# Moving the convolution steps of VectorE behind the masked copies in the recurrent heads

## The chip, the cores and the metric

One Trainium2 chip, of which the kernel uses one core. TensorE (PE) multiplies matrices into PSUM, VectorE (DVE), ScalarE (ACT) and GpSimd (POOL) do the elementwise work, and each engine works through its own list of instructions in the order in which the program wrote it; engines wait for one another through semaphores. The metric is device time in microseconds (us) of one execution; less is better.

## The reference, cut to what matters

Two transformer-like blocks on 1024 tokens of width 1024. The change touches the recurrent heads of the first block, eight heads of dimension 128, a gated delta rule in both directions of time:

```
qkv = silu(conv5(h @ w_in[:, q|k|v]))          # 5-tap convolution over time, per channel
q, k = l2norm(q), l2norm(k)
a_kk = strict_lower(kb @ k.T * gam)             # per chunk of 64 tokens
sol  = solve(a_kk + I, [v*beta, kb*exp(gc)])    # unit lower triangular
for chunk in chunks:                            # the scan
    v_new = u - w @ state
    o     = (q*exp(g)) @ state + a_qk @ v_new
    state = state*exp(g_last) + k.T @ v_new
out = rmsnorm(o) * silu(z)
```

The projections `h @ w_in` are by far the largest part of TensorE's work here.

## The kernel before, in words

The heads are worked through in 16 **halves**, numbered s = 2h + part: half s inverts the triangular matrices of four of the eight chunk pairs of head h. Meanwhile the same half prepares the next head (projections of q and k in an even half, of v and z in an odd one, their convolutions and norms), and runs scan steps of a head that is inverted. For the next heads 1 to 4 a half also projects gate columns of a later stage: in halves 0 to 7 (called **long** here) the preparation has 24 steps instead of 16; halves 8 to 13 are **short**; halves 14 and 15 prepare no head.

The inversion goes by levels. Level 0 sets up: TensorE multiplies k with k and q (L684), VectorE makes the matrix MT (L1178), TensorE transposes it (L694), and VectorE makes the two **masked copies** of level 0, called XT0 (L1183) and X0 (L1185), and then the masked attention product aq (L1192, two instructions). Level n = 1 to 6 then does, each step needing the one before:

- TensorE: product Y (L701), which needs X(n-1); ScalarE copies it out, Yb (L991)
- TensorE: product XT (L707), which needs Yb; ScalarE copies it out, Xb (L996)
- VectorE: first masked copy XTn (L1202)
- TensorE: transposes (L713), which need Xb; VectorE: second masked copy Xn (L1206)

The other work of VectorE in a half: the five convolution steps of each of q, k, v (one L1099 and four L1102 of 128x1024; the last of them signals `conv_sum`), then the final step (L1108), which needs ScalarE's tanh of the sum (L838) and signals `conv_out`, for which TensorE's flips (transposes, L644) wait; a split of loaded weights (L228, "ck" below) for which the next projection waits; z's product (L1114); the steps of the scan (L1219, L1227, L1237, L1240); and at the end of a head `fin`: a tiny L1247, which needs eight squares made by ScalarE (L1026), then GpSimd's power (L1329) and product (L1332), TensorE's transposes (L764), and VectorE's z0 and z1 (L1254), which free PSUM bank 5.

The order of the work on each engine is fixed when the program is built. `merged` interleaves the threads of a half (inv, prep, scan, fin, dec) by their number of steps, and `walk` issues one step of a thread's generator at each key of that list. All engines walk the same list:

```
for order in plan:
    walk(order, make)
```

So step i of "prep1" on ScalarE stands at the place of step i of "prep1" on VectorE, wherever the other threads' steps are. In an odd long half ScalarE's list reads: gate tanh (L860), tanh of k's convolution (L838, waits for `conv_sum` of k), from half 3 on the eight squares (L1026), then Yb of level 1 (L991), a copy of weights (L223), Xb of level 1 (L996). In an odd short half the tanh of k stands behind Xb of level 1.

Of the kernel before, what the change touches and what calls it, by code (L numbers as in the profile page):

```python
# [88 lines left out]
def walk(order, make):  # L89

    live = {}
    for key in order:
        if key not in live:
            live[key] = make(key)
        next(live[key], None)
    for g in live.values():
        for _ in g:
            pass


def idle(n):
    for _ in range(n):
        yield
# [17 lines left out]
def program(nc, x, wst, wab, cwt, vecs, gate, relb, meta, lam, lruw, cst, onehot, rope, msk, out):  # L121
    with ExitStack() as ctx:
# [654 lines left out]
        def both(first, second):  # L777
            yield from first
            yield from second
# [350 lines left out]
        def dve_prep0(v, h):  # L1130
            if h in GATES:
                yield from dve_next(v, CK[h, "g0"], h - 1)
            yield from dve_next(v, CK[h, "q"], h - 1 if h and h not in GATES else None)
            yield from conv_steps(v, h, "q", chq[h % 2])
            dve_ck(v, CK[h, "k"] + 1)
            yield
            yield

        def dve_prep1(v, h):
            q = h % 2  # L1140
            v.wait_ge(prep_ev, (h, "fq", 1))
            v.do.tensor_scalar(qe[h % 3], ssq[q], 128.0 * EPS, 128.0 * EPS * EPS, ALU.mult, ALU.add).then_inc(*dve_step.tick())
            yield from conv_steps(v, h, "k", chk[q])
            dve_ck(v, CK[h, "g1" if h in GATES else "v"] + 1)
            yield
            yield
            if h in GATES:
                yield from dve_next(v, CK[h, "v"])

            for n, _ in enumerate(conv_steps(v, h, "v", vf)):  # L1150
                if n == 0:
                    v.wait_ge(prep_ev, (h, "fk", 1))
                    v.do.tensor_scalar(ssk[q], ssk[q], 1.0, EPS, ALU.mult, ALU.add).then_inc(*unit_v.tick((h, "eps")))
                if n == 2:
                    v.wait_ge(gate_v, "beta")
                    v.wait_ge(gate_a, "egl")
                    v.wait_ge(unit_pow, h)
                    v.do.tensor_tensor(nk[q], ssk[q], rk, ALU.mult)
                    v.do.tensor_tensor(rk, rk, rk, ALU.mult).then_inc(*dve_step.tick())
                    v.wait_ge(dve_step, dve_step.n)  # L1160
                    for d in range(2):
                        v.do.tensor_tensor(br[q][d], gt["beta"][:, :, d * 8 + h], rk, ALU.mult).then_inc(*dve_step.tick())
                    v.wait_ge(dve_step, dve_step.n)
                    for d in range(2):
                        o = v.do.tensor_tensor(db[q][d], gt["dec"][:, :, d * 8 + h], br[q][d], ALU.mult)
                    o.then_inc(*unit_v.tick((h, "set")))
                yield
            dve_ck(v, CK[h, "z"] + 1)
            yield
            yield  # L1170
# [72 lines left out]
        def dve_fin(v, h):  # L1243
# [6 lines left out]
            for hf in range(2):  # L1250
# [3 lines left out]
                v.do.scalar_tensor_tensor(out=z, in0=bank(5), scalar=vc[:, NORMA:NORMA + 1], in1=z, op0=ALU.mult, op1=ALU.mult).then_inc(*fin_z.tick((h, hf)))  # L1254
                yield

        def dve_delta(v):
            def make(key):
                what, *of = key
                if what == "prep":  # L1260
                    return both(dve_prep0(v, 0), dve_prep1(v, 0))
                if what == "bias":
                    return idle(1)
                return {"qk": dve_qk0, "fill": dve_fill, "gates": dve_gates, "prep0": dve_prep0, "prep1": dve_prep1, "inv": dve_inv, "scan": dve_scan, "fin": dve_fin, "split": dve_first_split, "dec": lambda v, *_: idle(3)}[what](v, *of)

            for order in plan:
                walk(order, make)

# [2156 lines left out]
        @block.vector  # L3427
        def _(vector):
            v = Engine(vector)
            dve_input(v)  # L3430
            dve_delta(v)
            stage_ends(v, "dve", 1)
            dve_dilated(v)
            stage_ends(v, "dve", 2)
            dve_branches(v)
            stage_ends(v, "dve", 3)
            dve_rows(v)
            dve_ff(v)
            dve_lru(v)
            stage_ends(v, "dve", 6)  # L3440
            dve_rope(v)
            stage_ends(v, "dve", 7)
            dve_values(v)
            stage_ends(v, "dve", 8)
            dve_diff(v)
# [173 lines left out]
```

## Time and profile before

| | us |
|---|---|
| runs without the profiler, median of 3 | 3379.44 (3375.18 to 3379.78) |
| the profiled execution's own time | 3371.57 |
| its span, first to last instruction | 3369.8 |
| TensorE busy in the span | 3160.2 (94%) |
| VectorE busy | 1500.1 (45%) |
| ScalarE busy | 1054.8 (31%) |
| GpSimd busy | 361.4 (11%) |
| mean granted TensorE clock | 0.969 of full |

The page gives busy time of each engine, the waits say who waited for whom, the timeline lists instructions in order of time (runs of like ones merged), with the idle time before an instruction and what ended it in brackets, and the windows give busy time and granted clock of a stretch. The heads take the stretch from about 119 us to 1085 us. Matmul ends are modelled, so a busy TensorE isn't one at its peak; its idle time is real.

### The profile page before, as it was taken

To read this page: it belongs to the slowest core of one execution; us is meant where nothing else is said; L and a number is where in the kernel's file an instruction comes from. 1 tells how busy PE (TensorE), PEld (TensorE's weight loads), DVE (VectorE), ACT (ScalarE), POOL (GpSimd) and SP (SyncE) were. 2 spreads that over 40 slices of the span, in tenths; PEclk is the share of its full clock that TensorE was granted. 3 is DMA by queue.
4 is the path that set the end of the run, shared out by engine and by line. 5 is a ranking of instruction groups with operands and counts; after the bars stand their busy time and mean duration, and the time that the engine had idled before them with its cause. 6 is when DMAs were issued, how large, how long until landed. Compare 5 with 4: busy or idle time off the path is not lost.

```text
span 3369.8 us, 38831 instructions
## 1 busy us (share of the span) xinstructions
PE 3160.2 (94%) x16207; PEld 2575.5 (76%) x16207; DVE 1500.1 (45%) x2112; ACT 1054.8 (31%) x2290; POOL 361.4 (11%) x433
## 2 busy tenths in 40 slices
PE   7999999898899988989989999999999999998997
PEld 5788888777777877777744788888888877777876
DVE  4456556565643122121123345444444668533452
ACT  3544444444442223222300132222211333213452
POOL 0222232223221000000010000000000111001111
PEclk9999999999999999999999999999999999997998
DMA  2211111101111111101351321111111320111010
GB/s 105 66 55 45 48 48 45 32 32 38 32 38 57 57 35 49 49 29 44 122 206 67 150 73 57 50 42 46 50 51 50 107 78 26 62 38 45 26 39 26
DMA packets 59313, 194.86 MB, mean 58 GB/s; under 512 B 7649, under 2 KB 15329, under 8 KB 49410
## 3 DMA queue, kind: packets, MB, share of 16 engines
q1 hardware_dynamic: 58272, 191.29, 16.4%
q8 instruction: 128, 2.10, 0.3%
q10 hardware_dynamic: 866, 1.09, 0.1%
q14 instruction: 47, 0.39, 0.0%
HBM read 158.37 MB, written 33.98 MB: 57 GB/s over the span
## 4 chain that ended last, share of the span: by engine, by line
PE 80%; DVE 10%; ACT 6%; issue 2%; DMA 1%; POOL 1%; SPq 0%; ACTq 0%; DVEq 0%; POOLq 0%
PE ps L2308 18%; PE ps L2310 17%; PE ps L2309 17%; PE ps L2007 5%; PE ps L2185 3%; PE ps L701 3%; PE ps L707 3%; PE ps L1683 2%; PE ps L3186 2%; PE ps L744 1%; DVE ar L1102 1%; PE ps L1648 1%; PE ps L752 1%; PE ps L753 1%; PE ps L3143 1%
## 5 line engine op out<-in xcount | busy, mean ns | idle before, releaser
L2308 PE MATMUL ps<-r,r 128*128 128x512 f32 (+2 forms) x2656 | 1053.5, 397 | 37.2 <-DVE r L228 8.9
L2310 PE MATMUL ps<-r,r 128*128 128x512 f32 (+2 forms) x2656 | 1001.8, 377 | 0.0
L2309 PE MATMUL ps<-r,r 128*128 128x512 f32 (+2 forms) x2656 | 1000.4, 377 | 0.0
L2308 PEld LDWEIGHTS ps<-r,r 128*128 128x128 f32 x2656 | 513.0, 193 | 131.5 <-issue 17.8
L2310 PEld LDWEIGHTS ps<-r,r 128*128 128x128 f32 x2656 | 509.7, 192 | 94.1
L2309 PEld LDWEIGHTS ps<-r,r 128*128 128x128 f32 x2656 | 513.3, 193 | 80.7 <-issue 5.1
L2308 PE MATMUL ps<-r 128*128 128x512 f32 x512 | 199.8, 390 | 0.8 <-DVE r L2301 0.8
L2310 PE MATMUL ps<-r 128*128 128x512 f32 x512 | 199.4, 389 | 0.0
L2309 PE MATMUL ps<-r 128*128 128x512 f32 x512 | 199.4, 389 | 0.0
L2558 DVE TENSOR_TENSOR ar<-ar,ps 128x512 f32<-128x512 f32 x224 | 151.0, 686 | 92.1 <-PE ps L2310 92.0
L2007 PE MATMUL ps<-ar 128*128 128x512 f32 x384 | 170.9, 604 | 8.0 <-DMA ar<-sc_o 6.0
L2296 ACT ACTIVATE r<-ar 128x2048 fp32r<-128x2048 f32 x48 | 91.7, 1909 | 260.8 <-PE ps L2310 254.4
L1202 DVE COPY_PREDICATED ar<-mk,ar 128x512 f32<-128x512 uint8 x80 | 79.2, 990 | 162.4 <-ACT ar L996 162.4
L2007 PEld LDWEIGHTS ps<-ar 128*128 128x128 f32 x384 | 73.4, 194 | 99.2 <-issue 89.8
L701 PE MATMUL ps<-ar 128*128 128x128 f32 x768 | 110.2, 288 | 37.9 <-DVE ar L1185 23.1
L701 PEld LDWEIGHTS ps<-ar 128*128 128x128 f32 x768 | 100.1, 197 | 55.0 <-DVE ar L1185 28.4
L2301 DVE TENSOR_TENSOR r<-ar,r 128x2048 fp32r<-128x2048 f32 x48 | 112.1, 2336 | 34.7 <-ACT r L2296 34.7
L1102 DVE SCALAR_TENSOR_TENSOR ar<-ar 128x1024 f32<-128x1024 f32 x96 | 123.2, 1284 | 1.7
L1322 POOL TENSOR_SCALAR ar<-ar 128x128 f32<-128x128 f32 x128 | 96.4, 764 | 240.0 <-PE ps L744 240.0
L2512 DVE TENSOR_TENSOR ar<-ar 128x512 f32<-128x512 f32 x64 | 44.3, 692 | 173.6 <-ACT ar L2446 173.6
L991 ACT ACTIVATE ar<-ps 128x512 f32<-128x512 f32 x96 | 57.3, 596 | 198.2 <-PE ps L701 198.2
L2185 PE MATMUL ps<-ar 128*128 128x256 f32 x512 | 111.8, 380 | 1.6 <-DVEq L165 1.6
(319 smaller groups left out, 4257.2 us busy)
## 6 DMA issues: line engine op xcount, KB each, us to landing
ar<-wst SPq DMA_DIRECT2D x76, 1024.0 KB, 4.8
ar<-wst SPq DMA_DIRECT2D x52, 512.0 KB, 3.9
ar<-x SPq DMA_DIRECT2D x16, 512.0 KB, 10.3
ar<-sc_g SPq DMA_DIRECT2D x32, 256.0 KB, 4.7
sc_h<-ar SPq DMA_DIRECT2D x32, 256.0 KB, 2.0
sc_x<-ar SPq DMA_DIRECT2D x16, 512.0 KB, 2.8
ar<-sc_x SPq DMA_DIRECT2D x16, 512.0 KB, 4.2
sc_b<-ar SPq DMA_DIRECT2D x24, 260.0 KB, 2.0
```

The source lines that it names most:

```text
L701: o = t.do.matmul(q4(bank(4), j), q4(MT, j), mixed(FB0, b, j), start=True, stop=True)
L707: o = t.do.matmul(q4(bank(3), j), q4(Yb, j), mixed(BT, b, j), start=True, stop=True)
L1102: o = v.do.scalar_tensor_tensor(out=tmp, in0=r_[:, j:j + 1024], scalar=w[:, j:j + 1], in1=tmp, op0=ALU.mult, op1=ALU.add)
L1322: o = p.do.tensor_scalar(q4(kd[g % 2], d), q4(sqk[q], c), db[q][d][:, POS[c]:POS[c] + 1], None, ALU.mult)
L2007: o = t.do.matmul(br_bank(k), bv[:, kt, 128 * ct:128 * ct + 128], src[:, kt, hs], start=(kt == 0), stop=(kt == nk - 1))
L2185: o = t.do.matmul(bank(cb, 256), mT[:, kt, 128 * i:128 * i + 128], wv[:, kt, :], start=(kt == 0), stop=(kt == 7))
L2296: a.do.activation(w_set(j)[0], place, ACT.Copy).then_inc(*w_hi.tick(j))
L2301: v.do.tensor_tensor(lo, w_slot(W2 + j)[0], hi.bitcast(F32), ALU.subtract).then_inc(*w_lo.tick(j))
L2308: t.do.matmul(o, l[0], r[0], start=first, stop=False)
L2309: t.do.matmul(o, l[0], r[1], start=False, stop=False)
L2310: return t.do.matmul(o, l[1], r[0], start=False, stop=last)
L2558: v.do.tensor_tensor(dst, dst, bk, ALU.add).then_inc(*ff2_acc.tick(k))
```

## The change

VectorE alone walks another list; the other engines keep theirs. The new function goes through a half's list with n, the number of steps of the inversion so far. Steps of the preparation ("prep0", "prep1") are held back

- while n is 1, 2 or 3, until step 4 of the inversion (XT0, X0 and aq are one step) has been issued,
- after each first masked copy XTn of levels 1 to 5 (n = 6, 9, 12, 15, 18), until the second one, Xn, has been issued.

```
+        def dve_order(order):
+
+            held_, out_, n = [], [], 0
+            for key in order:
+                if key[0][:4] == "prep" and 0 < n < 22 and (n < 4 or n % 3 == 0 and n < 19):
+                    held_.append(key)
+                    continue
+                out_.append(key)
+                if key[0] == "inv":
+                    n += 1
+                    if n == 4 or n > 4 and n % 3 == 1:
+                        out_ += held_
+                        held_ = []
+            return out_ + held_
...
-                walk(order, make)
+                walk(dve_order(order), make)
```

Written out, the start of VectorE's list in three kinds of halves (m1 to m4 are the convolution's L1102 steps; s, o and x are scan steps):

```
odd long,   before: L1099+m1 | m2 | m3 | MT | m4 | XT0 X0 aq | fin L1247 | final | XT1 | ck | X1 | z0
            after:  L1099+m1 | MT | XT0 X0 aq | m2 | m3 | m4 | fin L1247 | final | XT1 | X1 | ck | z0
odd short,  before: L1099+m1 | m2 | MT | m3 | XT0 X0 aq | fin L1247 | m4 | XT1 | X1 | final | z0 | XT2 | ck | X2 | z1
            after:  MT | XT0 X0 aq | L1099+m1 | m2 | m3 | fin L1247 | m4 | XT1 | X1 | final | z0 | XT2 | X2 | ck | z1
even short, before: x | s,o | MT | x | z | XT0 X0 aq | s,o | XT1 ...   XT4 | s,o | m4 | X4 | XT5 | final | X5
            after:  x | s,o | MT | x | XT0 X0 aq | z | s,o | XT1 ...   XT4 | s,o | X4 | m4 | XT5 | X5 | final
```

Half 1 is odd long without a fin. In even long halves z moves from ahead of MT to behind aq, one ck from between XT1 and X1 to behind X1, and one convolution step from ahead of X4 to behind it. No instruction, no wait and no DMA is added or taken away; VectorE issues no DMA.

## Rows read from the trace of the kernel before

**Rows 1.** The page: busy time of each engine, share of the span, instructions.
```profile
PE 3160.2 (94%) x16207; PEld 2575.5 (76%) x16207; DVE 1500.1 (45%) x2112; ACT 1054.8 (31%) x2290; POOL 361.4 (11%) x433
```

**Rows 2.** Waits, 150 to 1070 us: who waited for whom, total, times, longest.
```profile
PE ps L701 <- DVE ar L1185: 23.1, 15, 2.7
...
PE ps L701 <- DVE ar L1206: 14.6, 16, 1.6
...
PE ps L2308 <- DVE r L228: 4.1, 3, 1.4
```

**Rows 3.** Timeline of PE in half 5 (odd long): start, duration, instruction.
```profile
418.73 0.60 PE L694 MATMUL ps<-ar 128*128 128x128 f32 x4
...
422.02 1.23 PE L701 MATMUL ps<-ar 128*128 128x128 f32 x8 [1.29 <-DVE ar L1185]
...
424.47 1.12 PE L707 MATMUL ps<-ar 128*128 128x128 f32 x8
...
430.21 0.50 PE L2308 MATMUL ps<-r,r 128*128 128x512 f32 x1 [1.40 <-DVE r L228]
```

**Rows 4.** Timeline of DVE in half 5.
```profile
418.32 1.27 DVE L1102 SCALAR_TENSOR_TENSOR ar<-ar 128x1024 f32<-128x1024 f32 x1
...
420.63 1.34 DVE L1185 COPY_PREDICATED ar<-mk,ps 128x512 f32<-128x512 uint8 x1
421.76 1.32 DVE L1192 TENSOR_TENSOR ar<-ps,ar 128x512 f32<-128x512 f32 x2
...
426.26 2.77 DVE L1202 COPY_PREDICATED ar<-mk,ar 128x512 f32<-128x512 uint8 x1 [1.90 <-ACT ar L996]
```

**Rows 5.** Timeline of ACT in half 5.
```profile
419.63 1.06 ACT L838 ACTIVATE ar<-ar 128x1024 f32<-128x1024 f32 x1
420.60 0.29 ACT L1026 ACTIVATE ar<-ar 128x128 f32<-128x128 f32 x1
...
423.29 0.60 ACT L991 ACTIVATE ar<-ps 128x512 f32<-128x512 f32 x1 [0.26 <-PE ps L701]
```

**Rows 6.** Timeline of POOL in half 5.
```profile
423.31 2.59 POOL L1329 TENSOR_TENSOR ar<-ar 128x8 f32<-128x8 f32 x1 [14.30 <-DVE ar L1247]
...
425.97 1.90 POOL L1332 TENSOR_TENSOR ar<-ar 128x1024 f32<-128x1024 f32 x1
```

**Rows 7.** Timeline of half 15, which prepares no head: DVE, then PE.
```profile
1007.08 1.29 DVE L1185 COPY_PREDICATED ar<-mk,ps 128x512 f32<-128x512 uint8 x1 [1.05 <-PE ps L694]
...
1008.42 1.23 PE L701 MATMUL ps<-ar 128*128 128x128 f32 x8 [1.38 <-DVE ar L1185]
```

**Rows 8.** Timeline of PE: half 9 (odd short), 10 (even short), 14.
```profile
659.90 0.60 PE L694 MATMUL ps<-ar 128*128 128x128 f32 x4
...
663.19 1.12 PE L701 MATMUL ps<-ar 128*128 128x128 f32 x4 [2.70 <-DVE ar L1185]
...
671.54 1.16 PE L701 MATMUL ps<-ar 128*128 128x128 f32 x8
...
678.47 0.60 PE L644 MATMUL ps<-ar 128*128 128x128 f32 x4
...
720.70 1.58 PE L701 MATMUL ps<-ar 128*128 128x128 f32 x8 [1.91 <-DVE ar L1185]
...
758.49 1.16 PE L701 MATMUL ps<-ar 128*128 128x128 f32 x8 [1.59 <-DVE ar L1206]
...
989.99 1.16 PE L701 MATMUL ps<-ar 128*128 128x128 f32 x8 [0.81 <-DVE ar L1206]
```

**Rows 9.** Timeline of DVE in the same halves.
```profile
677.59 0.74 DVE L1254 SCALAR_TENSOR_TENSOR ar<-ps,ar 128x512 f32<-128x512 f32 x1
...
717.09 1.21 DVE L1114 SCALAR_TENSOR_TENSOR ar<-ar 128x1024 f32<-128x1024 f32 x1
```

**Rows 10.** Windows in half 9: window, busy us of PE, PEld, DVE, ACT, POOL, granted clock, DMA share, GB/s.
```profile
663.00:666.00 3.00, 2.81 (x11) 2.62 (x12) 2.52 (x5) 0.60 (x1) 1.60 (x1) 0.55 0.00 0
666.00:669.00 3.00, 3.00 (x17) 2.58 (x16) 0.03 (x1) 1.26 (x3) 2.92 (x3) 0.88 0.00 0
```

## The prediction

> **What bounds the kernel now.** I read the page first: TensorE is busy for 94% of the span and VectorE for 45% [rows 1], so whatever VectorE does counts only where TensorE waits for it. The waits over the heads name those places, and the reader should see how small they are: 23.1 us in 15 waits of the first product Y for X0 (L1185), 14.6 us in 16 waits of later Y for Xn (L1206), 4.1 us in three waits of a projection for its split weights (L228) [rows 2]. The change can give back at most part of these 37.7 us and what the clock lost by them. The third view is the timeline, engine by engine, of a half of each kind. It repeats almost to 0.01 us between halves of a kind, so one half can be worked through and multiplied. The question to put to it is which engine stands in line behind a convolution step. The waits don't say so, since nobody waits long for one today.
>
> **The long second halves 3, 5 and 7, where I expect the loss.** In half 5 the last convolution step of k (L1102) starts at 418.32 and takes 1.27 [rows 4]; ScalarE's tanh starts at 419.63, right behind it [rows 5]. On ScalarE, whose order the change leaves alone, the tanh stands ahead of the eight squares and of Yb, and TensorE's next product XT (L707) needs Yb. So a convolution step held back on VectorE holds up ScalarE and then TensorE.
>
> After the change MT and XT0 come before the convolution steps. X0 still needs the transposes L694, which TensorE issues at 418.73 whatever VectorE does [rows 3]. Where VectorE is free, X0 starts as they end, 0.60 after their start [rows 7]; I count 0.63, so 419.36 instead of 420.63 [rows 4]. Y may then start 1.39 later (420.63 to 422.02), at 420.75, and TensorE was there at 422.02 - 1.29 = 420.73: the wait of 1.29 goes [rows 3, 4]. But aq starts 1.13 after X0 and takes 1.32, to 421.81; only then come three convolution steps of 1.28, to 425.65 instead of 419.59 [rows 4]. The tanh starts at 425.69, the first square 0.97 later, the squares end 2.43 after that (423.29 - 0.26 = 423.03, from 420.60), at 429.09, and Yb takes 0.60 and 0.05 to be seen [rows 5]. XT starts at 429.74 instead of 424.47: **5.3 us later** [rows 3]. TensorE is ready for it 2.45 after Y (422.02 to 424.47), at 423.2, and waits 6.5.
>
> Then the projection of v, which today waits 1.40 for the split ck [rows 3]: ck now has X1 ahead of it, 1.13 from start to start (as X0 and aq [rows 4]), with no slack to hide it. The long XT1 copy of 2.77, twice a level-0 copy of 1.34, runs into GpSimd's product of 1.90, which starts 0.29 before it [rows 4, 6]. That product starts 2.66 after the power, which follows fin's L1247. All of this moves by about 6, and the product now starts at about 432.0, just behind XT1 at 431.5 and ahead of X1 at 432.7. So the hold of some 1.4 moves from XT1 to X1 and ck stays behind it (bounds: gone, or twice). Behind so long a wait TensorE's clock also falls. In half 9, after a wait of 2.70 [rows 8], the granted clock is 0.55 and 0.88 in two windows of 3 us, 1.2 GHz for part of them: 1.7 us of full-speed time lost [rows 10]. Most of that hides under the wait for ck, but the product XT in the chain to XT1 is 0.5 to 0.9 slower. 5.3 + 1.1 + 0.5 = **6.9 us for each of three halves, 20.7** (bounds 5.0, with no hold left, and 8.5, with nothing of the clock hidden).
>
> The Trainium skill (PSUM — Partial Sum Buffer, Engine vs sequencer instructions) says that the queue of ScalarE is strictly first in, first out, which speaks against this change; the trace agrees, the tanh at 419.63 being followed by squares and Yb in list order. The Trainium skill (SBUF — State Buffer, Who interferes with whom) says that a VectorE instruction with at most one SBUF input doesn't contend with GpSimd outside the two-port modes; X1 reads its data from PSUM, so by that rule it would not be held, and the sum would be some 4 us smaller.
>
> **The first long second half, 1.** It has no fin, so the squares drop out: 5.3 - 2.4 = 2.9. Its projection doesn't wait for ck today (half 1 isn't among the three waits of [rows 2]), but has no slack either: 1.1, and 0.7 for the clock. **4.7** (3.8 to 6).
>
> **Long first halves 0, 2, 4, 6.** The wait for X0 is short there, 0.3, and one convolution step leaves the way of X4, worth 0.3 (0.6 in half 0). What moves behind is z, ck and that step. In halves 2, 4, 6 ck ends ahead of its projection, which comes after scan work: a **gain of 0.6 each, 1.8**. Half 0 has no scan: its projection starts the moment ck ends, so X1 ahead of it costs 1.2 against 0.6: **loss 0.6**.
>
> **Short first halves 8, 10, 12.** z (1.21 [rows 9]) leaves the way of X0, for which Y waits 1.91 [rows 8]; the transposes of MT then become the bound, so I take 0.9 (bounds 0 and 1.2). One convolution step leaves the way of X4: the wait goes from 1.59 to the 0.81 that half 14 has without any preparation [rows 8]. Against that, q's final step now stands behind X5, and the flips which wait for it come some 0.7 later. So 1.0 each. The drop of clock behind the 1.91 wait (Y takes 1.58 instead of 1.16 [rows 8]) should go in the two of three halves that have it, 1.6 each. **Gain 6.2** (1 to 8).
>
> **Short second halves 9, 11, 13.** The wait for X0 falls from 2.70 to the 1.38 of half 15 [rows 7, 8]. But four convolution steps and the first, tensor-scalar one are now behind aq. X0 at 659.90 + 0.63 = 660.53, aq over at 662.98, then 0.1 + 0.75 + 4 x 1.28 and the 0.15 of fin: 669.1. XT1 and X1 follow, 1.13 and 1.39, and the next Y starts at 671.6; today it starts at 671.54 without a wait [rows 8]. So the gain is used up, and TensorE now idles for 3 us just ahead of it, so that the low clock, hidden today, comes behind it: 1.4. GpSimd's product, needed by the flips L764, is later too, 0.3. And at level 2 ck passes X2 but not z1 (677.59), which gets 1.1 later; z1 frees bank 5 for the flips of k at 678.47, which start as z1 ends [rows 8, 9]: 1.0. Level 4 and level 5 cancel as above. **Loss 2.8 each, 8.4** (bounds 0 and 4 each).
>
> Halves 14 and 15 don't change. **Sum:** 20.7 + 4.7 + 0.6 + 8.4 - 1.8 - 6.2 = 26.4. The profiled execution took 3371.57 (span 3369.8, 1.8 around it), so 3398 for a profiled one. The median of the runs shown is 7.9 above it, so **3405 us**, 0.8% slower. About 0.2% (7 us) is what a measurement of this kernel can tell from no change.
>
> **Rivals.**
> 1. *The stalls go and nothing takes their place* (other side). Y's waits for X0 fall by 1.25 in four halves, 0.3 in three, 0.9 in three and 1.3 in three, 12.5 in all; those for X4 by 5; the clock keeps 5 x 1.6. That is 25.5: 3354. It needs ScalarE not to be held by the tanh, and decides itself where `conv_sum` of k comes before TensorE has finished Y, at 421.8 in half 5; the list puts it at 425.65. For it speak the 37.7 us of waits, against it tanh and last step, 0.04 apart [rows 4, 5]. Chance 0.06.
> 2. *Only Yb is late.* The hold is gone (X1 isn't held), ck slips into it, the clock doesn't fall in the short halves: 3 x 5.3 + 3.8 + 0.6, less 1.8 and 6.2, 12.3: 3392. For it: X1 reads PSUM. Chance 0.19.
> 3. *The clock isn't hidden.* Seven halves now have a wait of 3 to 6.5 us, and each loses 1.7 or more in full: 7 x 1.7 on top, 38: 3417. For it speaks that every wait of 2.7 here is followed by 1.2 GHz [rows 8, 10]; against it that TensorE then waits for ck anyway. Chance 0.15.
> 4. *The change does next to nothing*, losses and gains cancelling to within 7 us. It would take both the late Yb at its lower bound and the gains at their upper ones. Chance 0.03.
>
> **How the numbers follow.** The forecast has 0.57 (3397 to 3412 its own range). I leave rival 1 out, and rival 4 by its distance; 3388 to 3420 takes in rivals 2 and 3, but not their tails: about 0.8. Slower by over 0.2%: forecast, rival 2 and 3, 0.91; faster 0.06; same 0.03.
>
> **What would show it.** In the changed profile: in halves 3, 5, 7 the wait of L707 for Yb (L991) from nothing to about 6.5 us each, 4 in half 1, and tanh L838 waiting for L1102; the sum of Y's waits for X0 down from 23.1 to 10 or less; in the short second halves a wait of about 3 us of the level-2 Y for L1206; half 10 without a drop of clock. I'd be wrong if L707 did not wait there, if k's tanh stood elsewhere in ScalarE's list, or if more projection work could be issued ahead of L707.

## The result, and the profile after

The changed kernel takes 3403.1 us (median of 4 runs, 3402.0 to 3406.1) where the kernel before takes 3377.3 beside it: a ratio of 1.0084, interval 1.0071 to 1.0096. It is 25.8 us slower. The profiled execution took 3406.1 (span 3404.3).

The page of the changed kernel shows that TensorE has 0.4% more busy time for the same 16207 matmuls [rows 1]:

```profile
span 3404.3 us, 38831 instructions
...
PE 3171.6 (93%) x16207; PEld 2582.7 (76%) x16207; DVE 1513.0 (44%) x2112; ACT 1055.3 (31%) x2290; POOL 365.3 (11%) x433
```

The waits of the changed kernel over the same stretch as in [rows 2]:

```profile
ACT ar L838 <- DVE ar L1102: 37.9, 11, 7.9
...
PE ps L707 <- ACT ar L991: 31.7, 16, 6.2
...
PE ps L701 <- DVE ar L1206: 16.6, 15, 2.7
...
PE ps L701 <- DVE ar L1185: 10.2, 8, 1.9
...
PE ps L2323 <- DVE r L228: 8.8, 4, 3.0
```

And one of the kernel before:

```profile
PE ps L707 <- ACT ar L991: 9.3, 19, 0.9
```

Y's waits for X0 fell from 23.1 to 10.2, which is what the change was aimed at. But L707 now waits 31.7 us for Yb on ScalarE (24.4 of it in halves 1, 3, 5 and 7), and the first row says where that comes from: ScalarE's tanh waits 37.9 us for convolution steps of VectorE, a wait that no row of the kernel before has in this stretch. The projection's wait for ck has doubled (its L2308 is now L2323; GpSimd's and TensorE's later lines moved by 15).

The timeline of TensorE in the changed kernel, half 5 and then the level-2 product Y of halves 9 and 11:

```profile
428.94 1.89 PE L684 MATMUL ps<-ar 128*128 128x256 f32 x8
...
435.41 0.75 PE L701 MATMUL ps<-ar 128*128 128x128 f32 x4
...
444.26 2.07 PE L707 MATMUL ps<-ar 128*128 128x128 f32 x8 [6.23 <-ACT ar L991]
...
452.97 0.50 PE L2323 MATMUL ps<-r,r 128*128 128x512 f32 x1 [2.30 <-DVE r L228]
...
699.48 0.71 PE L701 MATMUL ps<-ar 128*128 128x128 f32 x4 [2.67 <-DVE ar L1206]
...
813.41 1.69 PE L701 MATMUL ps<-ar 128*128 128x128 f32 x8 [2.67 <-DVE ar L1206]
```

VectorE, in half 1 (first row) and half 5:

```profile
177.34 5.69 DVE L1102 SCALAR_TENSOR_TENSOR ar<-ar 128x1024 f32<-128x1024 f32 x3
...
434.05 1.31 DVE L1185 COPY_PREDICATED ar<-mk,ps 128x512 f32<-128x512 uint8 x1 [1.06 <-PE ps L694]
...
436.39 3.91 DVE L1102 SCALAR_TENSOR_TENSOR ar<-ar 128x1024 f32<-128x1024 f32 x3
...
447.00 2.74 DVE L1202 COPY_PREDICATED ar<-mk,ar 128x512 f32<-128x512 uint8 x1 [1.93 <-ACT ar L996]
449.54 1.35 DVE L1206 COPY_PREDICATED ar<-mk,ps 128x512 f32<-128x512 uint8 x1
450.69 2.22 DVE L228 TENSOR_TENSOR r<-ar,r 128x1024 fp32r<-128x1024 f32 x1
```

ScalarE in half 5:

```profile
440.33 1.06 ACT L838 ACTIVATE ar<-ar 128x1024 f32<-128x1024 f32 x1 [6.13 <-DVE ar L1102]
441.30 0.29 ACT L1026 ACTIVATE ar<-ar 128x128 f32<-128x128 f32 x1
...
443.63 0.57 ACT L991 ACTIVATE ar<-ps 128x512 f32<-128x512 f32 x1
```

GpSimd in half 1 (first row) and half 5:

```profile
177.50 4.44 POOL L1301 TENSOR_TENSOR ar<-ar 128x512 f32<-128x512 f32 x2 [11.43 <-DVE ar L1192]
...
446.67 1.90 POOL L1347 TENSOR_TENSOR ar<-ar 128x1024 f32<-128x1024 f32 x1
...
450.57 3.49 POOL L1301 TENSOR_TENSOR ar<-ar 128x512 f32<-128x512 f32 x2
```

This is one chain, read through four engines. The last of the convolution steps behind aq ends at 440.3; the tanh starts at 440.33; eight squares; Yb at 443.63; L707 at 444.26. Behind it XT1, X1 and ck follow each other without a gap, and the projection starts as ck is done. Counted from the half's first L684, L707 starts 15.32 us in (before 10.21) and the projection 24.03 (before 15.95).

Windows of the changed kernel, three in half 5, one in half 9 and one in half 11 (columns as in [rows 10]; the granted clock is the last but two):

```profile
441.00:444.00 3.00, 0.00 (x0) 0.00 (x0) 0.24 (x2) 3.00 (x18) 0.00 (x0) 0.64 0.00 0
444.00:447.00 3.00, 2.74 (x11) 2.55 (x12) 1.07 (x2) 1.75 (x3) 2.92 (x2) 0.50 0.00 0
447.00:450.00 3.00, 3.00 (x13) 2.39 (x12) 3.00 (x2) 0.00 (x0) 3.00 (x3) 0.73 0.00 0
...
699.00:702.00 3.00, 2.49 (x18) 2.06 (x19) 3.00 (x3) 0.72 (x2) 3.00 (x3) 1.00 0.00 0
...
813.00:816.00 3.00, 2.58 (x13) 2.35 (x14) 2.61 (x3) 0.66 (x2) 3.00 (x3) 0.64 0.03 8
```

TensorE stood idle up to 444.26 and its clock was at 1.2 GHz for the whole window behind that. Halves 9 and 11 have the same wait of 2.67; in 11 the clock fell behind it and in 9 it did not.

From the starts of L684 each half's length can be read and compared. These are differences to the kernel before in us, for the change and for the experiments that follow (profiled executions; a half ends where the next starts, so the sum runs to the start of half 15):

| half | 0 | 1 | 2, 4, 6 | 3 | 5 | 7 | 8 | 9 | 10, 12 | 11 | 13 | 14 | sum |
|---|---|---|---|---|---|---|---|---|---|---|---|---|---|
| predicted | 0.6 | 4.7 | -0.6 each | 6.9 | 6.9 | 6.9 | -1.0 | 2.8 | -2.6 each | 2.8 | 2.8 | 0 | 26.4 |
| the change | 0.4 | 7.4 | -1.2 each | 9.6 | 7.8 | 7.9 | -1.0 | 0.3 | -2.5 each | 1.6 | 1.7 | 0.0 | 26.9 |
| odd long halves as before | 0.4 | 0.0 | -1.2 each | 0.1 | 0.0 | 0.1 | -1.0 | 1.6 | -2.5 each | 1.6 | 0.4 | -1.6 | -7.2 |
| tanh behind Xb | 0.4 | 7.0 | -1.2 each | 6.0 | 5.0 | 6.2 | -1.0 | 0.4 | -2.6 each | 1.6 | 0.4 | -1.6 | 15.5 |
| level 0's rule only | 0.2 | 6.2 | -0.6 each | 6.2 | 5.9 | 6.1 | -0.9 | 1.1 | -2.5 each | -0.2 | 1.3 | -1.6 | 17.2 |
| levels 1 to 5 only | 0.3 | 0.9 | -0.6 each | 1.9 | 3.4 | 3.5 | 1.6 | 0.6 | -0.1, -1.6 | 0.4 | 0.6 | 0.0 | 9.7 |

The sum of the heads, 26.9, agrees with the difference of the medians, 25.8. The two spans differ by 34.5; the other 7.6 lie outside these halves, nearly all behind them, in stages that the change doesn't touch, and are less than the 8.8 by which runs of the kernel before differ among themselves.

### The profile page after: what moved, and what is told of

Its sections match the earlier page's. It is cut to its first block, busy times and chain, and to the rows that moved or that the text cites. A ratio compares the mean times of both kernels' runs of the same rounds, so it can differ in the third digit from the quotient of the medians.

```text
span 3404.3 us, 38831 instructions
## 1 busy us (share of the span) xinstructions
PE 3171.6 (93%) x16207; PEld 2582.7 (76%) x16207; DVE 1513.0 (44%) x2112; ACT 1055.3 (31%) x2290; POOL 365.3 (11%) x433
## 3 DMA queue, kind: packets, MB, share of 16 engines
q10 hardware_dynamic: 866, 1.09, 0.1%
## 4 chain that ended last, share of the span: by engine, by line
PE 81%; DVE 10%; ACT 5%; issue 2%; DMA 1%; POOL 1%; ACTq 0%; SPq 0%; POOLq 0%; DVEq 0%
PE ps L2323 18%; PE ps L2325 18%; PE ps L2324 18%; PE ps L2022 5%; PE ps L2200 3%; PE ps L707 3%; PE ps L701 2%; PE ps L1698 2%; PE ps L3201 2%; DVE ar L1102 1%; PE ps L744 1%; PE ps L752 1%; PE ps L753 1%; PE ps L1663 1%; PE ps L713 1%
## 5 line engine op out<-in xcount | busy, mean ns | idle before, releaser
L2323 PE MATMUL ps<-r,r 128*128 128x512 f32 (+2 forms) x2656 | 1056.5, 398 | 43.0 <-DVE r L228 14.8
L2323 PEld LDWEIGHTS ps<-r,r 128*128 128x128 f32 x2656 | 515.1, 194 | 138.6 <-issue 18.0
L2323 PE MATMUL ps<-r 128*128 128x512 f32 x512 | 199.7, 390 | 0.8 <-DVE r L2316 0.8
L2022 PEld LDWEIGHTS ps<-ar 128*128 128x128 f32 x384 | 73.3, 193 | 99.9 <-issue 89.7
L707 PE MATMUL ps<-ar 128*128 128x128 f32 x768 | 109.5, 288 | 32.8 <-ACT ar L991 32.4
L707 PEld LDWEIGHTS ps<-ar 128*128 128x128 f32 x768 | 102.8, 199 | 43.5 <-ACT ar L991 38.8
L701 PE MATMUL ps<-ar 128*128 128x128 f32 x768 | 106.7, 282 | 27.0 <-DVE ar L1206 16.6
L701 PEld LDWEIGHTS ps<-ar 128*128 128x128 f32 x768 | 99.1, 193 | 40.4 <-DVE ar L1206 21.8
L1102 DVE SCALAR_TENSOR_TENSOR ar<-ar 128x1024 f32<-128x1024 f32 x96 | 127.3, 1326 | 2.1
## 6 DMA issues: line engine op xcount, KB each, us to landing
ar<-x SPq DMA_DIRECT2D x16, 512.0 KB, 10.2
```

Source lines behind the costliest of these rows:

```text
L701: o = t.do.matmul(q4(bank(4), j), q4(MT, j), mixed(FB0, b, j), start=True, stop=True)
L707: o = t.do.matmul(q4(bank(3), j), q4(Yb, j), mixed(BT, b, j), start=True, stop=True)
L1102: o = v.do.scalar_tensor_tensor(out=tmp, in0=r_[:, j:j + 1024], scalar=w[:, j:j + 1], in1=tmp, op0=ALU.mult, op1=ALU.add)
L2022: o = t.do.matmul(br_bank(k), bv[:, kt, 128 * ct:128 * ct + 128], src[:, kt, hs], start=(kt == 0), stop=(kt == nk - 1))
L2323: t.do.matmul(o, l[0], r[0], start=first, stop=False)
```

## The experiments

**The old list in the odd long halves.** The change everywhere else.

```
+            if half in (1, 3, 5, 7):
+                return order
...
```

> The change, but halves 1, 3, 5 and 7 (long second halves) keep VectorE's old list. Theory (the loss is made where a convolution step of k is held back ahead of ScalarE's tanh, which stands ahead of Yb): the 32.6 us that these four halves lost go (7.4 + 9.6 + 7.8 + 7.9 between the starts of their k-q products), and what is left is the rest of the change, 6 us faster than the kernel before, ratio 0.998. The wait of L707 for L991 is gone in them. Rival (the loss comes from the level rule everywhere, ck and the final step behind the second copy): still at least 10 us slower than before.

Measured: 3368.25 us, ratio 0.9979 (0.9970 to 0.9988), as expected; the rival (still at least 10 us slower) is refuted. Halves 1, 3, 5 and 7 have their old lengths to 0.15 us (table). So more than the whole loss of the change sits in these four, 32.6, and what it does elsewhere is a gain, of 5.7 in the change's own run.

**ScalarE's tanh behind Xb.** The change, and in the odd long halves ScalarE walks a list in which the tanh of k and the copy behind it come after Xb of level 1.

```
...
+                if key[0] == "prep1":
+                    m += 1
+                    if m >= 5 and n < 6:
+                        held_.append(key)
+                        continue
...
```

> The whole change, and ScalarE's tanh of k moved behind Xb of level 1 in halves 1, 3, 5, 7 (with the copy of weights that follows it). VectorE's list is that of the change. Theory: Yb no longer stands behind the tanh, L707 waits for L991 by under 1 us there instead of 5.7 to 6.2; what stays is VectorE's own row, last step, tanh, final, XT1, X1, ck, so that the projection of v starts 1.5 us later than before in halves 3, 5, 7 and 3 to 5 in half 1. The heads lose about 4 us against before instead of 27: ratio about 1.001 (0.999 to 1.003). Rival (VectorE's row alone makes the loss, the tanh's place doesn't matter): within 5 us of the change, ratio 1.006 or more.

Measured: 3393.2 us, ratio 1.0057 (1.0043 to 1.0071). Neither the theory (about 1.001) nor the rival (within 5 us of the change) has it: the heads lose 15.5, against 26.9 in the change. The loss in halves 3, 5 and 7, 7.8 to 9.6 each, should have shrunk to about 1.5 and is 5.0 to 6.2; in half 1, where 3 to 5 were expected, it is 7.0 and hardly less than the change's 7.4. TensorE of this kernel in half 5, then VectorE:

```profile
433.62 1.12 PE L707 MATMUL ps<-ar 128*128 128x128 f32 x8
...
444.62 0.80 PE L2344 MATMUL ps<-r,r 128*128 128x512 f32 x1 [6.66 <-DVE r L228]
```

```profile
434.77 1.28 DVE L1122 SCALAR_TENSOR_TENSOR ar<-ar 128x1024 f32<-128x1024 f32 x1
...
437.26 1.23 DVE L1128 SCALAR_TENSOR_TENSOR ar<-ar 128x1024 f32<-128x1024 f32 x1 [1.13 <-ACT ar L838]
438.40 2.98 DVE L1222 COPY_PREDICATED ar<-mk,ar 128x512 f32<-128x512 uint8 x1
441.18 1.32 DVE L1226 COPY_PREDICATED ar<-mk,ps 128x512 f32<-128x512 uint8 x1
442.30 2.26 DVE L228 TENSOR_TENSOR r<-ar,r 128x1024 fp32r<-128x1024 f32 x1
```

L707 no longer waits for Yb, as the theory says. The wait comes back one step later, 6.66 for ck. VectorE's own row is the second chain: four convolution steps, the final step, XT1, X1 and ck stand in line, and with ScalarE out of the way they are the bound. Counted from the half's first L684 (424.69), the projection starts at 19.93, 4.0 later than before: XT1 starts 1.7 later, X1 stands ahead of ck (1.1), ck takes 2.26 beside GpSimd's addition (1.0, see below), and XT1 is held 0.2 longer. The other 1.0 of the half's 5.0 comes behind the wait of 6.66, where the clock is low (a first matmul of 0.80). Of the loss in halves 3, 5 and 7, 25.2 us, 8.0 go with ScalarE's order and 17.2 stay with VectorE's. So ScalarE's list is what binds in the changed kernel, but VectorE's own list stands close behind it and would have made two thirds of the loss by itself, and nearly all of it in half 1.

**One step behind the copies, with an error in the edit.** The kernel of this run doesn't do what its expectation says. The rule for n < 4 was taken out, but "n % 3 == 0" still held at n = 3 and let go only at n = 7, so the step between MT and level 0's copies was held past them and past X1. As `walk` issues a thread's steps in their order whatever places it is given, this makes everything behind that place one place later: the last convolution step of k stands behind aq, the final step behind X1 and ck behind the final step.

```
-                if key[0][:4] == "prep" and 0 < n < 22 and (n < 4 or n % 3 == 0 and n < 19):
+                if key[0][:4] == "prep" and 0 < n < 22 and n % 3 == 0 and n < 19:
...
-                    if n == 4 or n > 4 and n % 3 == 1:
+                    if n > 4 and n % 3 == 1:
```

> Only the second rule of the change (steps behind the second copy of levels 1 to 5); the steps of level 0 stay where they were before. Theory: the long second halves lose only what ck behind X1 costs, 1.1 to 2.3 us each; half 0 loses 0.5 as in the change; short second halves lose 0.8 each by ck ahead of z1 less 0.4 for the convolution step behind X4; even halves gain 0.3 to 0.5. In all 3 to 9 us slower than before, ratio 1.001 to 1.003, so some 20 of the 27 us hang on the first rule. Rival (ck behind X1 is the main loss): 15 us or more.

Measured: 3402.4 us, ratio 1.0088 (1.0074 to 1.0102). It can't decide between the rules. What it does show is that one place can cost as much as the whole change (27.5 us in the heads): L707 waits 3.60 for Yb in halves 3, 5 and 7, the projection 2.9 to 3.9 for ck, which has both X1 and the final step ahead of it, and these halves are 8.3 to 9.8 us longer.

**Levels 1 to 5 only,** with the edit as meant.

```
-                if key[0][:4] == "prep" and 0 < n < 22 and (n < 4 or n % 3 == 0 and n < 19):
+                if key[0][:4] == "prep" and 0 < n < 22 and n > 5 and n % 3 == 0 and n < 19:
```

> Edit: the reordering is kept only at levels 1 to 5 (a convolution step that the list has between a level's two masked copies goes behind the second); in front of level 0's copies everything stays as before. In the long second halves one step (the last convolution step of k) is then 1.1 us later, as X1 passes it. Theory (ScalarE's and VectorE's lists are strictly in order, every step in front of Yb and ck counts): halves 3, 5, 7 lose 1.2 to 2.3 us each, half 1 1.1, half 0 0.45, halves 9, 11, 13 0.4 each; halves 2, 4, 6 gain 0.5 and halves 8, 10, 12 0.2 each. In all +5.7 us against before, 1.0015 to 1.002. Rival (the level-0 rule isn't needed for the loss, one step that is late anywhere gives it in full): as the kernel of the last call, about 1.008.

Measured: 3387.2 us, ratio 1.0033 (1.0020 to 1.0045), 9.7 us where 5.7 were expected and the rival had 27. TensorE and VectorE in half 5:

```profile
425.29 1.12 PE L707 MATMUL ps<-ar 128*128 128x128 f32 x8
...
433.09 0.79 PE L2324 MATMUL ps<-r,r 128*128 128x512 f32 x1 [3.46 <-DVE r L228]
```

```profile
430.77 2.27 DVE L228 TENSOR_TENSOR r<-ar,r 128x1024 fp32r<-128x1024 f32 x1
```

L707 isn't late here, so this is the price of X1 ahead of ck by itself. The wait for ck goes from 1.40 [rows 3] to 3.46: 1.1 for X1, and 1.0 because ck, now later, runs beside GpSimd's L1301 and takes 2.27 where it takes 1.25 alone. In halves 5 and 7 the clock falls behind that wait (a first matmul of 0.79) and costs 1.5 more than in half 3. Half 8 is 1.6 longer for a like reason: its wait of 1.91 for X0 is that of the kernel before, but here the clock falls behind it. Without these three drops some 5 us are left, near the 5.7 of the theory. Half 3's 1.9 lies in its range of 1.2 to 2.3.

**Level 0's rule only.**

```
-                if key[0][:4] == "prep" and 0 < n < 22 and (n < 4 or n % 3 == 0 and n < 19):
+                if key[0][:4] == "prep" and 0 < n < 22 and n < 4:
```

> Edit: only the rule in front of level 0's copies is kept; at levels 1 to 5 the convolution steps stand between the copies as before. Theory (the loss comes from the four convolution steps that now stand behind aq): half 1 +6, halves 3, 5, 7 +6 to +8 each, halves 9, 11, 13 between -0.5 and +1 each; halves 2, 4, 6 gain 0.5, half 8 1.2, halves 10 and 12 2.7 each. In all about +20 us, 1.006. Rival (levels 1 to 5 carry half or more of it): 1.004 or less.

Measured: 3394.6 us, ratio 1.0056 (1.0040 to 1.0072), as expected (17.2 in the heads for about 20; the rival's 1.004 is the lower end of the interval). Half 5, TensorE:

```profile
440.97 2.08 PE L707 MATMUL ps<-ar 128*128 128x128 f32 x8 [6.25 <-ACT ar L991]
...
447.61 0.50 PE L2324 MATMUL ps<-r,r 128*128 128x512 f32 x1 [0.41 <-DVE r L228]
```

The wait of 6.2 for Yb belongs to level 0's rule alone, and the wait for ck nearly goes, as ck passes X1 again. The two parts add up, 17.2 + 9.7 = 26.9, though not half by half (the clock falls in different ones).

**GpSimd beside the convolution steps, first attempt.**

```
+                if part == 0 and 1 <= h <= 4:
+                    p.do.tensor_scalar(Eg[d], Eg[d], br[h % 2][d][:, 0:1], None, ALU.mult)...
```

> Edit: the change, and GpSimd's product of the masked decays for the first halves of heads 1 to 4 multiplies by one column (a tensor-scalar with one SBUF tensor in) where it multiplies two tensors (tensor_tensor); this changes what is computed there, the length of the tiles is the same. Theory (VectorE's convolution step and GpSimd's product hold each other over their second SBUF input): in half 1 three steps take 3.9 us in place of 5.69 and tanh waits 1.8 less, so half 1 is 1.8 us shorter; the split ck in halves 3, 5, 7 takes 1.24 in place of 2.22, 1.0 shorter each. In all about 5 us less than the change, 1.007 of before. Rival (the collision needs no second input, or it costs nothing on the path): the times of the change, 1.0085.

Measured: 3403.5 us, ratio 1.0081 (1.0064 to 1.0099): nothing, and no test of the theory. The edit hit an operation that stands elsewhere (at 219.98, 50 us into half 1, and not at 177, beside the convolution steps); three steps still take 5.69. (This kernel and the next compute something else than the reference in the places edited.) The operation that starts behind aq is the addition of the masks, `Eg[d] = rows[d] + mask`, L1301, which waits for `inv_dve` "aq". It was told from the wait in brackets of its row, which should have been read first.

**Second attempt, the addition.**

```
+                if part == 0 and 1 <= h <= 4:
+                    p.do.tensor_scalar(Eg[d], rows[d], 0.0, -10000.0, ALU.mult, ALU.add)...
```

> Edit: the run before aimed at the wrong operation; what starts behind aq and beside the convolution steps in half 1 (and beside ck in halves 3, 5, 7) is GpSimd's addition of the masks to the decay rows, two tensors in. Here the change, and that addition for the first halves of heads 1 to 4 made a tensor-scalar of the rows alone (times 0, minus 10000), so the decays of these halves are all 0 and their inverses the identity; the rest is untouched. Theory (VectorE and GpSimd hold each other where both read two SBUF tensors): in half 1 three convolution steps take 3.9 us in place of 5.69, tanh and Yb come 1.8 earlier and the half is 1.8 shorter; ck takes 1.24 in place of 2.22 in halves 3, 5 and 7, 1.0 shorter each. In all about 5 us less than the change, 1.007. Rival (any work of GpSimd holds VectorE, whatever its inputs): three steps still take over 5 us.

Measured: 3397.4 us, ratio 1.0063 (1.0049 to 1.0077). VectorE, then GpSimd, in half 1:

```profile
177.00 4.37 DVE L1102 SCALAR_TENSOR_TENSOR ar<-ar 128x1024 f32<-128x1024 f32 x3
```

```profile
177.17 3.13 POOL L1303 TENSOR_SCALAR ar<-ar 128x512 f32<-128x512 f32 x2 [11.45 <-DVE ar L1192]
```

The three steps take 4.37, against 5.69 beside the addition and 3.91 alone (half 5), and L707 in half 1 waits 4.36 in place of 5.68 (0.9 of this 1.3 reaches the length of the half). ck in half 5 takes 1.57 in place of 2.22. The theory had 3.9 and 1.24, the rival over 5, and neither is met.

The run doesn't show that the number of inputs matters, since the edit also made GpSimd's instruction shorter. All instructions of the line, in this kernel and in the changed one (shortest, median, longest in ns):

```profile
L1303 POOL TENSOR_SCALAR ar<-ar x8: 610/1574/1582, 177.2 to 577.0; 128x512 f32<-128x512 f32 x8
...
L1301 POOL TENSOR_TENSOR ar<-ar x32: 1262/1285/2280, 108.1 to 984.0; 128x512 f32<-128x512 f32 x32
```

One instruction unheld takes 0.61 in place of 1.26. Two of them are 1.3 us shorter, and that is the whole difference between 4.37 and 5.69; for ck, beside one of them, it is 0.65, the difference between 1.57 and 2.22. How the hold works can be seen in half 1 of the changed kernel, whose three steps and two additions start one after the other (second and third step, second addition):

```profile
178.65 4.38 DVE L1102 SCALAR_TENSOR_TENSOR ar<-ar 128x1024 f32<-128x1024 f32 x2
180.86 2.17 DVE L1102 SCALAR_TENSOR_TENSOR ar<-ar 128x1024 f32<-128x1024 f32 x1
...
179.70 2.24 POOL L1301 TENSOR_TENSOR ar<-ar 128x512 f32<-128x512 f32 x1
```

The second step comes while the first addition runs, and the first addition is over at 179.70; the second step is over at 180.8, the second addition at 181.94, the third step at 183.03. So one instruction ends every 1.1 us, alternately on VectorE and GpSimd, as if each ran only when the other's had ended. The same holds for XT1 and GpSimd's product: XT1 ends 1.17 after the product does (449.74 and 448.57), in the kernel before 1.16 after it (429.03 and 427.87), wherever in the product it started. So the size of the hold is about what the other engine's instruction has left to run. That a GpSimd instruction with one input holds less than one with two of the same length is not shown.

Halves 1, 5 and 7 are 0.9, 0.6 and 0.7 shorter than in the change; of half 3's 2.3, about 1.5 is the clock, which falls a second time there in the changed kernel and not in this one. Half 9 is 2.5 longer, where the clock falls behind the wait of 2.67, so that the heads lose 23.6 for 26.9.

**The rule only where it pays.** This version was put on record together with the first three experiments, so it was chosen by the waits of the kernels before and after alone: in even halves all of the rule but level 1 in half 0 and level 5 in the short ones; in the odd long halves nothing; in the odd short ones, in front of level 0's copies all but the first step of the preparation, and of the levels only level 4.

```
...
+                    early = 0 < n < 4 and (not odd or not long_ and m > 1)
+                    late = n % 3 == 0 and 3 < n < 19 and (not odd and not (half == 0 and n == 6) and not (not long_ and n == 18) or odd and not long_ and n == 15)
...
```

> The rules applied only where the traces show a wait of TensorE and nothing behind the held step: no holding in long second halves; even halves as in the change but ck stays ahead of X1 in half 0 and the final step ahead of X5 in short ones; in short second halves the first preparation step stays ahead of MT, two convolution steps go behind aq, the last one behind X4, ck and the final step stay. Theory: 0.9 us gained in half 0, 1.25 in each of 2, 4, 6, 1.7 in 8, 3.3 in 10 and 12, 1.7 to 3.3 in 9, 11, 13: 17 to 21 us faster than before, ratio 0.994 to 0.995. Rival (gains at one wait come back at the next, as in the short second halves of the change): under 7 us, ratio over 0.998.

Measured: 3354.3 us, ratio 0.9946 (0.9933 to 0.9960), as expected (20.4 us for 17 to 21) and faster than both kernels. The odd short halves, a loss in the change, are 2.7 to 2.8 us shorter than before; halves 3, 5 and 7 as before.

**Two lists in the odd long halves.** The version above, with the last convolution step of k behind aq on VectorE (`or long_ and m > 3`) and the tanh between Yb and Xb on ScalarE.

> Edit: the rule where it pays (as in the version run before) and, in the long second halves 1, 3, 5 and 7, the last convolution step of k alone goes behind aq on VectorE, while ScalarE's tanh of k goes behind Yb of level 1 and the copy that follows it behind Xb of level 1. Theory (the wait of Y for X0 was the convolution step, and the loss was ScalarE's list): Y's wait of 1.3 us in halves 1, 3, 5 and 7 goes, L707 doesn't wait for Yb, the projection of v waits no longer than before: 6 to 9 us less than the version where it pays, 3346 to 3349, ratio about 0.9925. Rival (the step comes back as a wait of the projection for ck, since k's final copy is now later): no gain over 0.9945, and the wait for ck grows from 1.4 to 2.5 or more.

Measured: 3353.7 us, ratio 0.9933 (0.9921 to 0.9946), against 3354.3 and 0.9946 for the version above, timed on another occasion: the intervals overlap, and the theory's 6 to 9 us are not there. The lengths of the halves decide: without half 14, where the clock fell in one profile and not in the other, this version gains 18.8 and the one above 20.9. So the rival is right that the step comes back as a wait for ck, though that wait grows to 1.97 and not to its 2.5. TensorE in half 5, then VectorE:

```profile
418.66 1.23 PE L701 MATMUL ps<-ar 128*128 128x128 f32 x8 [0.31 <-DVE ar L1208]
...
427.42 0.77 PE L2353 MATMUL ps<-r,r 128*128 128x512 f32 x1 [1.97 <-DVE r L228]
```

```profile
423.25 2.98 DVE L1225 COPY_PREDICATED ar<-mk,ar 128x512 f32<-128x512 uint8 x1
```

Y's wait for X0 falls from 1.29 to 0.31, and 0.6 of it comes back as a longer wait for ck (1.97 for 1.40). The rest, and more, goes to the clock: TensorE's first matmul behind the wait takes 0.77 (0.50 in [rows 3]) and halves 3 and 5 are 1.1 to 1.2 longer than in that version; half 7, with the same wait, keeps its clock and is 0.4 shorter. XT1 takes 2.98 here, held by GpSimd's product.

**GpSimd's product behind ck.** The version where it pays, and:

```
...
+            if h < 3:
+                p.wait_ge(in_lo, CK[h + 2, "g1" if h + 2 in GATES else "v"] + 1)
             p.do.tensor_tensor(o3, o3, per_chunk(sso[q], 8), ALU.mult).then_inc(*fin_on.tick(h))
```

> Edit: the version where it pays, and GpSimd's product behind the power (the normed output of the finished head) waits in halves 3, 5 and 7 for VectorE's split ck. Theory (the wait of the v projection for ck, 1.40 us in halves 3, 5 and 7, is the 1.4 us that this product holds XT1): XT1 takes 1.34 in place of 2.76, ck ends 1.4 earlier, the projection doesn't wait, 1.3 shorter each: 4 us less than the version where it pays, 3350, ratio 0.9933 or, against its measured 0.9946 on the other chip job, 0.0012 less. Rival (the product is late for the flips L764 behind it, or holds the key scaling of the scan): no gain, a new wait of TensorE for GpSimd.

Measured: 3352.2 us, ratio 0.9927 (0.9914 to 0.9939), as the theory has it. VectorE in half 5 (XT1, X1):

```profile
421.84 1.31 DVE L1202 COPY_PREDICATED ar<-mk,ar 128x512 f32<-128x512 uint8 x1 [1.90 <-ACT ar L996]
...
424.12 1.31 DVE L1206 COPY_PREDICATED ar<-mk,ps 128x512 f32<-128x512 uint8 x1
```

And GpSimd:

```profile
424.34 1.90 POOL L1356 TENSOR_TENSOR ar<-ar 128x1024 f32<-128x1024 f32 x1 [2.88 <-DVE r L228]
```

X1 and the product now run side by side, and neither is held. XT1 takes 1.31, the projection doesn't wait at all, and halves 3, 5 and 7 are 1.4 to 1.5 us shorter than before. Nobody waits for the product. The ratio is 0.0019 below the version where it pays; the two were timed on different occasions.

**Both moves.**

> Edit: as the kernel with the product behind ck, and in halves 3, 5 and 7 also the last convolution step of k alone behind aq, with ScalarE's tanh of k between Yb and Xb of level 1 and the copy that follows it behind Xb. Theory: Y's wait for X0 falls from 1.3 to 0.3, XT1 isn't held, so ck ends in time and TensorE's clock stays up: halves 3, 5 and 7 2.3 shorter each than in the version where it pays, 7 us in all, 3347. Rival (with k's final copy 2 us later ck is the end of the chain, whoever holds XT1): the wait for ck is 0.5 or more and the gain no larger than that of the product's move alone.

Measured: 3346.2 us, ratio 0.9912 (0.9900 to 0.9925), the fastest. TensorE in half 5:

```profile
415.30 1.23 PE L701 MATMUL ps<-ar 128*128 128x128 f32 x8 [0.33 <-DVE ar L1208]
...
422.31 0.50 PE L2355 MATMUL ps<-r,r 128*128 128x512 f32 x1 [0.22 <-DVE r L228]
```

Y's wait is 0.33, the wait for ck 0.22, and the clock stays up. Halves 3, 5 and 7 are 2.0 to 2.1 us shorter than before, some 2.1 shorter than in the version where it pays (expected 2.3). The moved step that brought nothing alone brings 0.6 per half once ck has slack. The intervals of this kernel and the one without the step overlap (0.9912 and 0.9927), so that the 0.6 is real is read from the half lengths, which agree in all three halves with the clock at full in both. They explain 1.8 us; the medians are 6.0 apart, and no trace shows where the rest comes from.

## Why the prediction came out as it did

The median came out 2 us below the 3405 forecast and inside the range. The place was as forecast, and so was the way in which L707 gets late. That the sum of 26.4 meets the 26.9 of the profile is luck: against the forecast the three long second halves lost 4.5 more and half 1 lost 2.7 more, while the short second halves lost 4.8 less and the long first halves gained 1.9 more. What the forecast didn't say is that VectorE's own list, without any help of ScalarE's, would make most of the loss.

- *The tanh holds up Yb and L707.* Forecast 5.3 us later in halves 3, 5 and 7, wait 6.5; measured 5.1 and 6.23. The kernel with the tanh moved shows the cause: L707's wait goes. It also shows what the cause is worth, 8.0 of the 25.2 us in these halves and 0.4 of 7.4 in half 1, because the convolution steps, XT1, X1 and ck on VectorE then hold up the projection.
- *ck behind X1 and the hold.* Forecast: the hold moves from XT1 to X1, and the step costs 1.1. Measured: from XT1's start to the projection 5.97 in place of 3.95, so 2.0. 1.1 of it is X1. The hold stayed on XT1 (2.74 beside L1347), because XT1 was later than I had it relative to the product, 0.3 behind it and not 0.5 ahead: I had put 0.5 for the low clock ahead of XT1 into the sum, but not into XT1's start at 431.5, and it is 0.95. By the turns seen above XT1 would not have waited for a product that starts behind it, so that a hold was met here for a wrong reason. And ck got a second one, 1.0, from L1301, which the prediction had not counted. X1, which reads its data from PSUM, isn't held: in the changed kernel it takes 1.35 and doesn't meet the product, and where it does, with the product moved behind ck, it takes 1.31 and the product 1.90. By the rule of the Trainium skill (SBUF — State Buffer, Who interferes with whom) that was to be so; the trace agrees, and my assumption that the hold passes to X1 was wrong.
- *The clock ahead of XT1.* Forecast 0.5, measured 0.95 from L707 to XT1. With these three, 5.1 + 0.95 + 2.0 = 8.1 for the projection; 0.3 is won back behind it in halves 5 and 7. Half 3 has another 1.6: there the clock falls again behind the wait of 2.99. The term for the three halves was 20.7 and measured 25.2.
- *Half 1.* Forecast 4.7 (to 6), measured 7.4. L707 is 4.5 later and not 2.9, since three convolution steps take 5.69 beside L1301. The run with the shorter instruction in place of L1301 took 1.3 of that hold away. The steps were priced by rows in which GpSimd was idle, and moved to where it isn't. The other error is the clock, forecast 0.7: six projection matmuls of 0.63 to 0.77 us stand between L707 and the transposes, so that XT1 is 0.95 later and X1 waits another 1.09 for L713, a wait which the hold on XT1 hides in the other three halves.
- *Odd short halves.* Forecast 8.4, measured 3.6. The wait of 2.67 for X1 (forecast 3) and that of 0.76 for z1 (forecast 1.0) are there, and in halves 11 and 13 the clock falls behind the first. In half 9 it didn't, and as a drop of before went too, the half is level. I had charged the drop to all three in full. Which of the three the clock falls in changes from run to run (half 9 with the shorter L1301), and no trace shows what decides it.
- *Even halves.* Short ones forecast -6.2, measured -6.0, with no drop of clock in 10 and 12. Long ones forecast -1.8, measured -3.7: X0 and X4 each give back 0.3 more than their wait. The profile shows only part of such a wait as idle time: a matmul of 0.40 is followed by the next one after 0.23 where nothing is waited for, so the 0.17 of overlap is lost with the wait, and the eight products behind it take 1.16 to 1.23 in place of 1.05 to 1.12. Half 0 +0.4 for +0.6.

Rival 1 fails at the place it named: `conv_sum` came at 440.3, long after Y. Rival 2 was right that X1 isn't held, but wrong that the hold goes: XT1 takes 2.74, ck 2.22, and the projection waits 2.3 to 3.0 for ck. Rival 3 fails in its size: the drop behind L707's wait is hidden under the wait for ck, as forecast, and a drop shows in full only in half 3 and in halves 11 and 13.

## What to carry to other kernels

When one engine's list is reordered and the others keep theirs, look at what each of the others has in line behind the result that gets later: here the product that waited longest, L707, has no use for the moved step. Then look at what the reordered engine's own list has behind it, for that chain can be nearly as long: with ScalarE's list put right, two thirds of the loss in halves 3, 5 and 7 stayed. Price a moved instruction by what runs beside it in its new place, not by its row in the old one; on VectorE that means looking at GpSimd's list at that time. And a step moved to fill a wait brings nothing while the next wait has no slack; give that one slack first (here the GpSimd product behind ck), and the same move pays.

## What the runs showed of the hardware

- VectorE's convolution steps (two SBUF tensors in) and GpSimd's additions took turns: three steps of 128x1024 take 3.91 us alone and 5.69 beside two additions of 128x512, which themselves take 4.44 for 2.53 elsewhere (half 2), and an instruction of one or the other ends every 1.1 us. Beside two tensor-scalar instructions, of 0.61 each in place of 1.26, they take 4.37. Both sides pay, each about what the other's instruction has left to run.
- ck, a 128x1024 subtraction, takes 1.25 alone and 2.22 to 2.27 beside that addition; the masked copy XT1 1.31 alone and 2.74 to 2.98 beside GpSimd's product of 1.90. The masked copy X1, with its data in PSUM, takes 1.31 beside the same product: it isn't held.
- Whether the clock falls behind a wait of about 2 to 3 us isn't fixed by the half: after the same wait of 2.67 it fell in halves 11 and 13 and not in 9, and half 14, whose work is the same in every kernel here, is 1.6 us shorter in some of them than in others. Such a drop is worth 1.5 us, so lengths of single halves can't be told apart below that unless the granted clock is the same in both.
